# Griffin and sparse attention step on one core: value products and transposes ahead of the projection ticks, probability copies ahead of the next exponential

## What is computed

```python
z = rmsnorm(x, p['norm_mix']) @ p['w_in']                 # the projection
# attention, for a block of 128 queries and each head: three softmaxes
lc = q . kc * scale + bias      # "cmp": 63 compressed keys
ls = q . ks * scale + bias      # "sel": all keys up to the block, 128 to 1024
lw = q . kw * scale + bias      # "win": a window, 128 to 640 keys
o = g0 * softmax(lc) @ vc + g1 * softmax(ls) @ vs + g2 * softmax(lw) @ vw
# recurrence, for each channel
a = exp(-8 * sigmoid(xr @ w_a + b_a) * softplus(-lam))
b = sqrt(-expm1(2 * log_a)) * (sigmoid(xr @ w_i + b_i) * xc)
h = scan(a, b);  out = h * gelu(gate)
```

## Time and profile before

| | us |
|---|---|
| median of 3 runs | 2672.07 (2669.81 to 2676.27) |
| the profiled execution | 2671.46 |
| its span in the trace | 2669.8 |
| PE busy in it | 2416.7 (91%) |
| DVE busy | 1072.0 (40%) |
| ACT busy | 724.7 (27%) |
| POOL busy | 655.0 (25%) |

### The profile page before, as it was taken

One profiled execution on the slowest core, in us unless ns is written; L12 is line 12 of the kernel. 1 busy time (PEld: TensorE's weight loads), 2 busy tenths in 40 slices (PEclk: granted clock), 3 DMA queues, 4 the chain that ended last, 5 costly groups with the idle time before them and its releaser, 6 DMA issues. The chain is left out here.

```text
span 2669.8 us, 37831 instructions
## 1 busy us (share of the span) xinstructions
PE 2416.7 (91%) x14415; PEld 2234.0 (84%) x14415; DVE 1072.0 (40%) x1945; ACT 724.7 (27%) x1319; POOL 655.0 (25%) x399
## 2 busy tenths in 40 slices
PE   7996877989989899899856587999999999999999
PEld 7995647789888788799733577999999999999999
DVE  5465014436255564655433003263333333333333
ACT  5222011242352544644332004232211111111111
POOL 2212001111111011010035001234444434433443
PEclk9997789999999899999678568999999999999999
DMA  5224424224233221110056626332111111111112
GB/s 178 88 80 168 125 72 147 67 67 128 64 97 88 74 63 52 60 49 28 6 125 181 160 65 246 104 119 91 61 48 47 40 47 47 47 39 47 47 47 79
DMA packets 136151, 226.26 MB, mean 85 GB/s; under 512 B 29418, under 2 KB 95098, under 8 KB 135420
## 3 DMA queue, kind: packets, MB, share of 16 engines
q1 hardware_dynamic: 122492, 194.57, 23.5%
q0 software_dynamic: 6560, 25.22, 3.2%
q10 hardware_dynamic: 6976, 4.79, 0.7%
HBM read 176.80 MB, written 55.08 MB: 87 GB/s over the span
## 5 line engine op out<-in xcount | busy, mean ns | idle before, releaser
L1101 PE MATMUL att_facc<-h_hi,att_w_hi 128*128 128x344 f32 x960 | 337.7, 352 | 57.8 <-DVE att_zf L1281 44.5
L2153 PE MATMUL tl_acc<-tl_x_hi,tl_w_hi 128*128 128x344 f32 x1632 | 348.0, 322 | 21.1 <-DVE tl_x_lo L2216 14.0
L2153 PE MATMUL tl_acc<-tl_x_lo,tl_w_hi 128*128 128x344 f32 x1632 | 347.2, 321 | 0.0
L2153 PE MATMUL tl_acc<-tl_x_hi,tl_w_lo 128*128 128x344 f32 x1632 | 345.4, 320 | 0.0
L1101 PE MATMUL att_facc<-h_lo,att_w_hi 128*128 128x344 f32 x960 | 314.5, 328 | 0.0
L1101 PE MATMUL att_facc<-h_hi,att_w_lo 128*128 128x344 f32 x960 | 314.2, 327 | 0.0
L2153 PEld LDWEIGHTS tl_acc<-tl_x_hi,tl_w_hi 128*128 128x128 f32 x1632 | 275.2, 189 | 22.5 <-issue 15.9
L2153 PEld LDWEIGHTS tl_acc<-tl_x_lo,tl_w_hi 128*128 128x128 f32 x1632 | 277.0, 189 | 0.0
L2153 PEld LDWEIGHTS tl_acc<-tl_x_hi,tl_w_lo 128*128 128x128 f32 x1632 | 272.6, 188 | 0.0
L2118 POOL TENSOR_TENSOR tl_w_lo<-tl_raw,tl_w_hi 128x1024 fp32r<-128x1024 f32 x64 | 153.9, 2404 | 425.1 <-ACT tl_w_hi L2059 425.1
L1101 PEld LDWEIGHTS att_facc<-h_hi,att_w_hi 128*128 128x128 f32 x960 | 187.7, 196 | 72.4 <-DVE att_zf L1281 42.2
(11 more groups left out here) (355 smaller groups left out, 4031.5 us busy)
## 6 DMA issues: line engine op xcount, KB each, us to landing
tl_raw<-in_w_ff SPq DMA_DIRECT2D x66, 512.0 KB, 3.6
z<-att_zf SPq DMA_DIRECT2D x120, 172.0 KB, 3.7
att_raw<-in_w_in SPq DMA_DIRECT2D x40, 512.0 KB, 4.3
tl_tmp<-z SPq DMA_DIRECT2D x24, 516.0 KB, 4.4
tl_raw<-in_w_up SPq DMA_DIRECT2D x16, 512.0 KB, 4.0
fr_raw<-in_w_in SPq DMA_DIRECT2D x14, 512.0 KB, 4.8
zn<-fr_x SPq DMA_DIRECT2D x10, 516.0 KB, 2.9
fr_x<-in_xT SPq DMA_DIRECT2D x8, 644.0 KB, 10.3
```

What stands on the lines that cost most here:

```text
L1101: mm = pe.matmul(facc[:, 0:CW], w[:, u % 2, k, :], h[:, k, c * CW:(c + 1) * CW], start=(x == 0), stop=(x == 23))
L2153: mm = pe.matmul(a[:, c, 0:CW], wt[:, s, k, :], x[:, x0, c * CW:(c + 1) * CW], start=first and n == 0, stop=last and n == 2)
```

## The change

In each step of the three loops the same calls are made in another order. On PE the ticks of a step go from ahead of `values` and `transposes` to behind them. On ACT `copies(J)` and the output turns go ahead of `probs(J + 1)`. On DVE `evict` goes from the first place of a step to behind `accumulate`, `maxima` and `coefficient`, and `accumulate` goes ahead of `maxima`. No instruction is added or removed; no buffer and no wait is changed.

```diff
@@ block.tensor, for J in range(NST)
                     scores(J + 1)
                     if J + 1 in gate_at:
                         gate_products(J + 1)
-                for tick in ticks[J]:
-                    filler(tick)
                 if J >= 1:
                     values(J - 1)
                 transposes(J)
@@
                     turn(J // NJ, 0)
                 if J % NJ == 2 and J >= NJ:
                     turn(J // NJ - 1, 1)
+                for tick in ticks[J]:
+                    filler(tick)
             values(NST - 1)
@@ block.scalar, for J in range(LAST)
                 if J < NST:
-                    if J + 1 < NST:
-                        probs(J + 1)
                     copies(J)
                     if J % NJ == 8:
                         turned(J // NJ, 0)
                     if J % NJ == 2 and J >= NJ:
                         turned(J // NJ - 1, 1)
+                    if J + 1 < NST:
+                        probs(J + 1)
                     for u in range(2, NU):
                         if unit_at[u - 2] == J:
                             w_high(u)
@@ block.vector, for J in range(LAST)
+                if 2 <= J < NST + 2:
+                    accumulate(J - 2)
+                if J < NST:
+                    maxima(J)
+                if 1 <= J <= NST:
+                    coefficient(J - 1)
                 for g in range(3 * NU):
                     if chunk_at[g] + 1 == J and J:
                         evict(g)
-                if J < NST:
-                    maxima(J)
-                if 2 <= J < NST + 2:
-                    accumulate(J - 2)
-                if 1 <= J <= NST:
-                    coefficient(J - 1)
```

## The result

The changed kernel takes 2683.93 us (median of 20 runs, 2679.76 to 2689.81), the kernel before 2672.43 on the same chip (20 runs); the ratio is 1.0037, with an interval of 1.0027 to 1.0047. By the medians it is slower by 11.5 us, by the ratio 9.9. I had forecast 2670 and gave this direction 0.26. The profiled execution has a span of 2678.7 us, 8.9 longer than before.

What follows compares the result with a forecast made beforehand. PE was taken to bound the joined program, with 72 of 908 us in named waits. The terms -7.7 - 2.7 + 0 + 4.0 + 2.8 + 1.5 gave -2.1 on 2671.5, so 2670 as median; range 2657 to 2685.

Steps and rivals of the forecast that it cites:

- Part 4: Steps without ticks: each sel transposes wait 2.4 us, 0.7 more for each of six rounds; costs 4.0 us.
- Rival C: Clock of the steps without ticks moves from 0.68: about 10 us faster or 7 slower; chance 0.10.
- if the clock without ticks left 0.6 to 0.75: Steps without ticks: a clock outside this range would show the forecast wrong.
- rounds of 9.0 to 9.1: Steps without ticks: expected sign, rounds this long in us with one wait of 2.4 at each sel transposes.
- Part 6: Ends: first step's transposes wait +2.2 us, masked probabilities save 0.7; costs 1.5 us.
- rival B: Blocks 3 to 7: recurrence pieces make maxima late at 40 sel steps, 14 us more, 2684; chance 0.20.
- Parts 1 and 2: Blocks 1 and 2, four ticks a step: shorter evict waits save 7.7 us, a higher clock 2.7.
- part 2: Clock in blocks 1 and 2: half of 5.5 us of slowed matmuls behind waits is given back; saves 2.7 us.
- Parts 3 and 5: Blocks 3 to 6: recurrence steps in 3 to 5 change nothing; sel steps behind one tick cost 2.8 us.
- a sum near 30: Blocks 3 to 5: expected sign, copies and exponentials named as releasers, waits summing near 30, where it was 27.
- A: Blocks 3 to 5: the recurrence's waits halve as well, 9.5 us less, 2660; chance 0.20.
- Part 1: Blocks 1 and 2, four ticks a step: evict waits of 13.4 us fall to 5.7; saves 7.7 us.

Runs made afterwards that it cites:

- n4: The changed kernel with 12 unused matmuls ahead of the transposes of each sel step from 174 on: 2657.91 us.
- n13: The order of n3 with 6 unused matmuls ahead of the transposes of each sel step: 2667.18 us.
- n3: The kernel before with the new order only from step 173 on, where there are no ticks: 2682.69 us.
- n12: The changed kernel with maxima ahead of accumulate, evict behind the recurrence's piece, and in step 0 PE's ticks ahead of transposes: 2663.95 us.
- n1: The kernel before with the new order only in steps 24 to 71 (blocks 1 and 2): 2665.97 us.

## Why the prediction was wrong

| part | place | predicted | measured |
|---|---|---|---|
| 1 and 2 | blocks 1, 2 | -10.4 | -10.8 |
| 3 and 5 | blocks 3 to 6 | +2.8 | +1.9 |
| 4 | no ticks | +4.0 | +12.2 |
| 6 | block 0 | +1.5 | +7.7 |

**Part 4 is the step that failed**: "With the mix behind 0.68 I take 0.7 for each of six rounds". The wait was priced right: 2.4 foretold, 2.0 to 2.4 measured, and the row of all such waits, 1259 to 1345 us, stands against the 9.4 of the earlier trace rows:

```profile
PE att_tp L1064 <- ACT att_pr L1139: 13.2, 6, 2.4
```

With 1.1 for the copies that are still waited for, that is 4.9 us more in six rounds, 0.8 each, close to my 0.7. The other 7.3 us of the 12.2 are PE's busy time. I held the mix of the two levels fixed, as if it were a property of the stretch, and it belongs to the waits: the wait of before was cut into pieces of up to 1.5 us, and most rounds had some high time; the one of 2.0 to 2.4 gave three quarters of each round to 1.2 GHz. n4 (clock 1.00, the same order on DVE and ACT, 58.5 us), n13 (0.85, 67.1 us) and n3 (0.63, 83.1 us) show that the loss goes with the clock. Rival C saw the place, but priced the whole way down to 0.5 at 7 us, from the difference between a mean round and an undisturbed one. The measured fall of 0.07 alone cost that. My test "if the clock without ticks left 0.6 to 0.75" was therefore useless: it stayed inside, at 0.63, and the forecast was wrong all the same. The sign that did tell was "rounds of 9.0 to 9.1": they take 13.2 to 13.7. And I took the one round of 8.59 as the rule to add to, though it was the fastest of its stretch.

**Part 6 failed too**: "the mask waits for values, accumulate and maxima of the next step, 1.3". It is 2.5 to 2.8 at three steps, and the seven are 12.5 in all for 10.3, since I left out what stands between an evict and the next `accumulate` on DVE. I knew of such pieces (rival B is built on them), but looked for them from block 3 on, with sel, and not in block 0. The +2.2 for the first step was right as a wait (2.58 at 430.02), and lacked the clock behind it; by its trace n12 gives the step 4.6.

**Parts 1 and 2 were right** in size and mechanism. In blocks 1 and 2 the waits other than the mask's are 3.3, 2.7 and 0.3, together 6.3 where 5.7 was foretold, in place of 13.4; the clock rose from 0.97 to 0.99 and PE's busy time fell by 2.9 us, for the 2.7 of part 2; n1 has the gain alone. In two names they were off: at the places behind `w_high`, priced at 2.4 and 2.6, PE waits 1.9 and 2.0, but more than half of it at values, for `accumulate`, and no longer for evicts. Which of the three moves (ticks, copies, evict) brings this gain, no run tells apart.

**Parts 3 and 5 were right as a sum, less so in their names.** By block the sum is -3.2, +2.4, +2.0 and +0.5 (blocks 3 to 6), with 0.3 for the steps up to 174. PE's waits from 840 to 1259 us sum to 29.0, for "a sum near 30":

```profile
PE att_tp L1064 <- ACT att_pr L1139: 14.5, 18, 1.8
PE att_O L1083 <- DVE att_oacc L1325: 11.9, 3, 5.7
PE att_O L1083 <- DVE att_oacc L1322: 2.6, 2, 2.3
```

Copies are not among them. I had named a copy, waiting for the sigmoids, as the long wait. It is `accumulate`, which stands behind the product that waits for the sigmoids; the values need `O` to be free:

```profile
888.82 1.23 DVE L1353 TENSOR_TENSOR att_ri<-att_ri,att_xc 128x1032 f32<-128x1032 f32 x1 [6.56 <-ACT att_ri L1178]
889.22 1.28 ACT L1139 ACT_TABLE_LOAD   x1
889.97 0.28 DVE L1325 SCALAR_TENSOR_TENSOR att_oacc<-att_O,att_cf,att_oacc 128x64 f32<-128x64 f32 x1
...
890.30 1.33 PE L1083 MATMUL att_O<-att_v_sel,att_ptr 128*128 128x64 f32 x5 [5.71 <-DVE att_oacc L1325]
...
891.35 0.69 ACT L1139 ACTIVATE att_pr<-att_S,att_nmx 128x512 f32<-128x512 f32 x1 [0.85 <-DVE att_nmx L1300]
```

The same rows answer for the table load that moved: it ends at 890.50, and the exponential then waits 0.85 for its maxima, so it is hidden, as the sum had it. The Trainium skill ("ScalarE: Activation LUTs", What ACT_TABLE_LOAD costs) would add 1380 ns of drain; that is more than the 0.85 and would have shown, and does not: the exponential starts 0.04 behind the end of its maxima (890.62 and 0.69).

**The rivals.** A did not come: blocks 3 to 6 got 1.9 longer. B ended nearest to the time (2684), by chance: its 14 us in blocks 3 to 7 were to come from late maxima, and blocks 3 to 6 lost 1.9 and block 7 by the clock. Its mechanism, a recurrence piece ahead of `accumulate`, is real, but it cost time in block 0; the long waits that it makes in blocks 3 to 5 took the place of evict waits as long. C was the right place with too small a price.

**Sums of the prediction.** Six times 0.7 is 4.2, not 4.0 (part 4). Seven mask waits of 1.3 for 10.3 us (the 15.8 of the earlier trace rows less the eighth, 5.5) save 1.2, not 0.7 (part 6). Part 1 counts PE's way to the same transposes once as 5.95 and once as 5.3, and only the first has its terms; with it the wait of 2.4 would be 1.75. In C six times 2.1 is 12.7, not some 10. Together this moves the forecast by less than 1 us.

**What stays open**: which of the moves in blocks 1 and 2 is worth what, what ACT's order is worth in the steps without ticks, and how much of block 0's clock each of its waits costs.

## What to carry to other kernels

Where a stretch runs between the two levels of the clock, its level is not a constant to multiply by: here 4.9 us more of waiting, gathered into one wait a round, came with 7.3 us of slower matmuls, and the cheapest check is a run with unused matmuls in the gap. On an engine that works through its list in order, as DVE does here, put the calls that feed the next step (here the maxima) ahead of those that wait for another engine's present work (here `accumulate`), and list for every moved wait what stands behind it in that engine's queue, in all stages. An order that gains in one stretch (-10.8 us in blocks 1 and 2) can lose in another with as much cover (+7.7 in block 0) and in one with none (+12.2), so look at each stretch by itself and let the order change with it; n8 keeps the old one in block 0, has the maxima first behind it, and gains 1.3%.

## What was not expected of the hardware

Adding work to TensorE made the kernel faster: 72 matmuls more, and 2657.91 us instead of 2683.93, since the granted clock of that stretch went from 0.63 to 1.00. Waits of 2.0 to 2.4 us, one in each round of small f32 matmuls, came with 0.63; waits of 0.9 to 1.2 (and six more matmuls a round) with 0.85; waits of 0.6, with no matmuls added, with 1.00. At the low level the eight transposes of 128x128 took 1.97 us for 1.09.
